# Trainium2, one core: the second block's projection by seven half-width products instead of eight full-width blocks, with weight sums and row scaling on GpSimd

## What is computed

```python
def second_block(x, ...):
    x = x + 0.5 * swiglu(rms_norm(x, ffn1_norm[l]), ...)
    h = rms_norm(x, mix_norm[l])
    proj = h @ w_in[l]                      # 1024 -> 3600 columns
    qkv_a, z_a, a_a, b_a, qkv_b = jnp.split(proj, split_at, axis=-1)
    o_a = gdn_mixer(qkv_a, z_a, a_a, b_a, conv_w[l], ...)   # conv of 5, silu, l2 norm of q and k, delta rule
    o_b = dilated_mixer(qkv_b, q_norm_w[l], k_norm_w[l], rel_bias[l])  # rms norm of q and k, band attention
    x = x + jnp.concatenate([o_a, o_b], axis=-1) @ w_out[l]
    x = x + 0.5 * swiglu(rms_norm(x, ffn2_norm[l]), ...)
```

## Time and the profile before

| | |
|---|---|
| median of three runs | 3348.02 us (3344.82 to 3357.39) |
| the profiled execution, device time | 3344.23 us |
| its span in the trace | 3342.5 us |
| projection stage, first product to first logits | 2383.86 to 2607.40 us |
| PE busy | 3122.7 us, 93% |
| DVE / ACT / POOL busy | 1938.0 / 870.7 / 316.2 us |

### The profile page before, as it was taken

How to read it: one execution, slowest core, us unless ns; L and a number is a source line. 1 busy time by engine, 2 the same in 40 slices (tenths; PEclk the granted TensorE clock), 3 DMA queues, 4 the chain that set the end, 5 groups by cost and what they waited for, 6 DMA issues and landing times.

```text
span 3342.5 us, 72507 instructions
## 1 busy us (share of the span) xinstructions
PE 3122.7 (93%) x28246; PEld 2282.4 (68%) x28247; DVE 1938.0 (58%) x3738; ACT 870.7 (26%) x1541; POOL 316.2 (9%) x277
## 2 busy tenths in 40 slices
PE   8998999799989998999699979999999799999997
PEld 5445886577765446885577758888644478588886
DVE  1486674456651676663566677664548666476644
ACT  1116110356651134111466630000111522110000
POOL 1000000322230000001322210000000033000000
PEclk9999999899999999999899979999999999999998
DMA  7110324299952112223599822223253000122231
GB/s 283 62 65 1 126 89 162 110 341 380 376 193 104 56 45 76 89 88 128 193 377 377 337 107 84 87 89 100 93 110 121 12 3 3 55 84 89 89 97 68
DMA packets 83479, 446.85 MB, mean 134 GB/s; under 512 B 19888, under 2 KB 20024, under 8 KB 39616
## 3 DMA queue, kind: packets, MB, share of 16 engines
q1 hardware_dynamic: 55200, 377.51, 30.4%
q0 software_dynamic: 25136, 63.49, 6.0%
q10 hardware_dynamic: 2928, 3.07, 0.3%
HBM read 411.00 MB, written 32.89 MB: 133 GB/s over the span
## 4 chain that ended last, share of the span: by engine, by line
PE 87%; DVE 4%; ACT 4%; issue 3%; DVEq 1%; DMA 1%; POOL 0%; ACTq 0%; POOLq 0%
PE pb L1150 24%; PE pb L724 17%; PE pb L1030 10%; PE pb L891 9%; PE pb L1053 5%; PE pb L931 4%; PE pb L985 3%; PE pb L1466 2%; ACT arena L1494 1%; PE pb L760 1%; PE pb L828 1%; PE pb L871 1%; PE pb L1037 1%; PE pb L1011 1%; PE pb L1342 1%
## 5 line engine op out<-in xcount | busy, mean ns | idle before, releaser
L1150 PE MATMUL pb<-arena,streamed 128*128 128x256 f32 x1952 | 446.9, 381 | 5.8 <-DVE arena L2335 5.0
L1150 PEld LDWEIGHTS pb<-arena,streamed 128*128 128x128 f32 x1952 | 372.8, 191 | 59.0 <-issue 6.3
L1030 PE MATMUL pb<-arena,xT 128*32 x3008 | 351.6, 276 | 18.1 <-issue 11.4
L724 PE MATMUL pb<-xT,streamed 128*128 128x512 f32 x832 | 365.9, 598 | 0.0
L1030 PE MATMUL pb<-streamed,xT 128*32 128x128 f32 x9024 | 354.7, 276 | 5.8 <-issue 5.8
L1030 PEld LDWEIGHTS pb<-arena,xT 128*32 128x32 f32 x3008 | 323.4, 111 | 32.5 <-issue 26.8
L1030 PEld LDWEIGHTS pb<-streamed,xT 128*32 128x32 f32 x9024 | 327.0, 111 | 7.9 <-issue 7.9
L724 PEld LDWEIGHTS pb<-xT,streamed 128*128 128x128 f32 x832 | 158.5, 192 | 198.4 <-issue 198.2
L1620 ACT ACTIVATE streamed<-arena 128x3072 f32 x94 | 260.1, 2767 | 56.4 <-SPq L483 37.8
L1150 PE MATMUL pb<-arena,am 128*128 128x256 f32 x976 | 227.3, 379 | 0.0
L1150 PEld LDWEIGHTS pb<-arena,am 128*128 128x128 f32 x976 | 185.4, 190 | 25.2
(11 more groups left out here) (459 smaller groups left out, 4967.9 us busy)
## 6 DMA issues: line engine op xcount, KB each, us to landing
arena<-in_w_moe SPq DMA_DIRECT2D x192, 1024.0 KB, 9.4
streamed<-in_w_tail SPq DMA_DIRECT2D x87, 1024.0 KB, 5.0
streamed<-in_w_layer SPq DMA_DIRECT2D x78, 1024.0 KB, 4.9
xT<-xs_dram POOLq DMA_DIRECT2D x22, 512.0 KB, 8.5
ys_dram<-xT POOLq DMA_DIRECT2D x88, 128.0 KB, 9.2
xs_dram<-lnw POOLq DMA_DIRECT2D x12, 512.0 KB, 17.7
rel_dram<-xtok POOLq DMA_DIRECT2D x1, 4092.0 KB, 86.7
arena<-rel_dram POOLq DMA_DIRECT2D x1, 3584.0 KB, 15.2
```

The source lines that it names most:

```text
L724: last = mm(pb[bank][:, 0:cols], unit(w, u, k), rhs[:, k * cols:(k + 1) * cols], start=(k == 0), stop=(k == KC - 1))
L1030: last = mm(pb[m][r0:r0 + MOE_BLOCK, 0:FW], rows, w, start=(k == 0), stop=(k == KC - 1))
L1150: last = mm(pb[p][:, 0:HALF], stat(i), mov(i), start=(opens and i == 0), stop=(closes and i == steps - 1))
```

## The change

The projection's 28 groups become 14 pairs, one weight pair each. PE makes seven products a pair, each of four steps with 128x256 inputs: P1 = a11 and P2 = a12 into the halves of bank 0, P3 (weights s2) and P4 (a21, changed in place) into bank 1, P5 (s1) and P6 (s4) into bank 6, P7 (a22) into bank 7. P3 waits for the first and P4 for the second signal of the weight sums.

- POOL forms the weight sums (`in_weights`: four operations of 128x512). They have one set of buffers, so those of pair c+1 wait until P6 of pair c is done. It also multiplies each recombined pair by `rs` (`scale_pair`, 128x1024), which was DVE's L2527. The silu, squares and convolutions wait for it.
- ACT copies the first half bank of each pair (`first_product`), DVE recombines by seven adds of 128x256 (`in_reads`, `in_upper`).
- The input sums are made by DVE inside the last part of the feed-forward (`projection_sums`).
- The norm sums go by batches of four groups: PE makes four products with 32 columns of ones into four row ranges of bank 2, ACT takes the root of one 128x512 tile, DVE one reciprocal of it (`invert`), PE spreads it to banks 2 to 5 by four products over 32 rows, and DVE multiplies by the banks (`apply_norm`). `n_done` counts to 4. The first sums stand in pair 4 between P4 and P5, the first spread in pair 5 at the same place; the further ones follow every second pair.
- The bias table's load `hank` is issued by POOL after `scale_pair(10)` instead of straight behind its store; the store follows `scale_pair(1)`. The copy of v by ACT moves behind the last pair, and PE waits for it ahead of the fourth logits.

On POOL (the DMAs of the bias table stand where the text above says):

```diff
-            pool.wait_ge(n_done, 2)
+            def in_weights(c):
...
+                pool.wait_ge(w_loaded[j % SLOTS], (DEPTH * LAYER_USES + j // SLOTS + 1) * 16)
+                if c:
+                    alone(pool)
+                    pool.wait_ge(prod_ready, IN_PRODS + N_PROD * (c - 1) + 6)
+                add(s1, a21, a22, ALU.add)
+                pool.drain()
+                add(s2, s1, a11, ALU.subtract).then_inc(w_summed, 1)
+                add(a21, a11, a21, ALU.subtract)
+                pool.drain()
+                if c == 0:
+                    pool.wait_ge(sq_summed, 2)
+                add(s4, a12, s2, ALU.subtract).then_inc(w_summed, 1)
...
+            def scale_pair(c):
+
+                pool.wait_ge(prod_read, IN_READS + 4 * c + 4)
+                y = cut(in_pair(c), S)
+                nc.gpsimd.tensor_tensor(y, y, rs.unsqueeze(1).to_broadcast([P, 2, S]), ALU.mult).then_inc(lin_free, 2)
...
+            in_weights(0)
+            for c in range(IN_PAIRS):
+                if c + 1 < IN_PAIRS:
+                    in_weights(c + 1)
+                if c == 0:
+                    pool.wait_ge(ab_scaled, 1)
+                    alone(pool)
+                scale_pair(c)
```

On PE:

```diff
-            pe.wait_ge(dn_free, KC)
+            pe.wait_ge(prod_read, products_read(0, FF_SUMS))
...
-            for g in range(H_AB):
-                linear(pair(AB_SLOT + 1 + g // 2), g % 2, xns[1], DEPTH * LIN_LAYER + g, g % 2)
...
-                    mm(pb[2 + c % 4][:], ones if c < 8 else block_ones, nsq[c % 2], start=True, stop=True).then_inc(nsum_ready, 1)
...
+                b = (g - 8) // 4
+                if g % 4 == 0 and 0 <= b < 4:
+                    pe.wait_ge(rvar, 2)
+                    pe.wait_ge(nsq_ready, 4 * (b + 1))
+                    alone(pe)
+                    if b:
+                        pe.wait_ge(n_done, b)
+                    for q in range(4):
+                        last = mm(pb[SUM_BANK][q * 32:q * 32 + 32, :], ones[:, 0:32] if b < 2 else block_ones[:, 48:80], nsq[q], start=True, stop=True)
+                    last.then_inc(nsum_ready, 1)
+                b = (g - 10) // 4
+                if g % 4 == 2 and 0 <= b < 4:
+                    pe.wait_ge(n_inverse, b + 1)
...
+                    for q in range(4):
+                        r0 = q * 32
+                        last = mm(pb[2 + q][:], (pick_row if b < 2 else pick_rows)[r0:r0 + 32, :], nrm[b][r0:r0 + 32, :], start=True, stop=True)
+                    last.then_inc(n_spread, 1)
...
+                bank_free(0)
+                product(0, 0, a11, part(0, 0))
+                product(0, 1, a12, part(1, 0))
+                pe.wait_ge(w_summed, IN_SUMS + 2 * c + 1)
...
+                product(1, 0, s2, added(1))
+                pe.wait_ge(w_summed, IN_SUMS + 2 * c + 2)
...
+                product(1, 1, a21, added(2))
+                at_group(2 * c)
+                bank_free(2)
+                product(6, 0, s1, added(0))
+                product(6, 1, s4, part(1, 1))
+                sums_ready(4)
+                bank_free(3)
+                product(7, 0, a22, added(3))
+                at_group(2 * c + 1)
```

On ACT, in step g (with silu of group g - 2 between the first piece and the second):

```diff
+            def first_product(c):
+
+                if c:
+                    act.wait_ge(prod_read, IN_READS + 4 * (c - 1) + 2)
+                    alone(act)
+                act.wait_ge(prod_ready, IN_PRODS + N_PROD * c + 2)
+                fn(in_first, pb[0][:, 0:HALF], ACT.Copy).then_inc(first_copied, 1)
...
+                if g % 2 == 0 and 0 < g < H_AB:
+                    first_product(g // 2)
...
+                    if c >= 4:
+                        act.wait_ge(nsum_ready, c // 4)
+                    elif c == 2:
+                        act.wait_ge(rel_ready, 1)
+                    fn(nsq[c % 4], grp(big, c), ACT.Square).then_inc(nsq_ready, 1)
...
+                    act.wait_ge(nsum_ready, b + 1)
+                    fn(nrm[b], pb[SUM_BANK][:], ACT.Sqrt, scale=1.0 if b < 2 else 1.0 / HEAD_DIM, bias=eps).then_inc(nstd, 1)
```

On DVE:

```diff
+            def in_reads(c):
+
+                dve.wait_ge(first_copied, 2 * DEPTH * MIXED + c + 1)
+                alone(dve)
+                out = in_pair(c)
+                p1, u2, u3 = in_first, in_u2, in_u3
+                v.tensor_tensor(out[:, 0:HALF], p1, pb[0][:, HALF:S], ALU.add).then_inc(prod_read, 1)
+                dve.wait_ge(prod_ready, IN_PRODS + N_PROD * c + 4)
+                v.tensor_tensor(u2, p1, pb[1][:, 0:HALF], ALU.add)
+                dve.drain()
+                v.tensor_tensor(u3, u2, pb[1][:, HALF:S], ALU.add).then_inc(prod_read, 1)
+
+            def in_upper(c):
...
+                dve.wait_ge(prod_ready, IN_PRODS + N_PROD * c + 6)
...
+                dve.wait_ge(prod_ready, IN_PRODS + N_PROD * c + 7)
+                v.tensor_tensor(out[:, S:3 * HALF], u3, pb[7][:, 0:HALF], ALU.add).then_inc(prod_read, 1)
...
-                    dve.wait_ge(lin_ready, DEPTH * LIN_LAYER + g + 1)
-                    v.tensor_tensor(grp(big, H_ORDER[g]), pb[g % 2][:], rs, ALU.mult).then_inc(lin_free, 1)
-                    dve.drain()
+                    if g % 2 == 0:
+                        in_reads(g // 2)
+                    else:
+                        in_upper(g // 2)
+                    dve.drain()
...
+                if g - 2 < H_SQ or g in V_AT:
+                    dve.wait_ge(lin_free, DEPTH * LIN_LAYER + 2 * (g // 2) + 2)
+                    alone(dve)
+                    convolve(g - 2 if g - 2 < H_SQ else H_V + V_AT.index(g))
+                b = g // 4 - 2
+                if g % 4 == 1 and 0 <= b < 4:
+                    invert(b)
+                if g % 4 == 3 and 0 <= b < 4:
+                    apply_norm(b)
```

More of the change, by code:

```diff
@@ L277, in two_blocks @@
         ctmp = [pT2[0], pT2[1]]
[L278 to L279 removed]
+        nsq = lg2[0:2] + [am[:, 2 * S:3 * S], am[:, 3 * S:4 * S]]
+        nrm = [am[:, 3072 + (b % 2) * S:3072 + (b % 2 + 1) * S] for b in range(4)]
+        pick_row, pick_rows = am[:, S:S + P], am[:, S + P:S + 2 * P]
         at[0] = 0
@@ L650, in _ @@
-            pool.wait_ge(n_done, 2)
+            def in_weights(c):
+                j = AB_SLOT + 1 + c
+                s1, s2, s4 = in_w
+                w = ring[j % SLOTS]
+                a11, a12, a21, a22 = (w[:, q * S:(q + 1) * S] for q in range(4))
+                add = nc.gpsimd.tensor_tensor
+                pool.wait_ge(w_loaded[j % SLOTS], (DEPTH * LAYER_USES + j // SLOTS + 1) * 16)
[10 more added lines that the diff above has]
+                add(s4, a12, s2, ALU.subtract).then_inc(w_summed, 1)
@@ new lines, in apply_norm @@
+            def apply_norm(b):
+                dve.wait_ge(n_spread, b + 1)
+                for q in range(4):
+                    x = grp(big, 4 * b + q)
+                    last = v.scalar_tensor_tensor(out=x, in0=x, scalar=(P ** -0.5, 1.0, qk_w[:, 0:1], qk_w[:, 1:2])[b], in1=pb[2 + q][:], op0=ALU.mult, op1=ALU.mult)
+                last.then_inc(n_done, 1)
+            def in_reads(c):
[6 more added lines that the diff above has]
+                v.tensor_tensor(u2, p1, pb[1][:, 0:HALF], ALU.add)
+                dve.drain()
+                v.tensor_tensor(u3, u2, pb[1][:, HALF:S], ALU.add).then_inc(prod_read, 1)
@@ new lines, in _ @@
+            picks = identity.rearrange("p (q r) -> p r q", r=32)
+            for r in range(2):
+                v.tensor_reduce(pick_rows[:, r * 64:r * 64 + 1], picks[:, 16 * r, :], AX.X, ALU.add)
+            v.tensor_scalar(qk_w[:, 0:1], qk_w[:, 0:1], HEAD_DIM ** -0.5, None, ALU.mult)
+            dve.drain()
+            v.tensor_copy(pick_row, pick_rows[:, 0:1].to_broadcast([P, P]))
+            for r in range(2):
+                v.tensor_copy(pick_rows[:, r * 64 + 1:r * 64 + 64], pick_rows[:, r * 64:r * 64 + 1].to_broadcast([P, 63]))
```

224 lines of the change are left out of this document (135 added, 89 removed).

## The result

The changed kernel takes 3423.1 us (median of 4 runs, 3422.6 to 3429.0) against 3352.7 us for the kernel before beside it (4 runs): ratio 1.0223, interval 1.0201 to 1.0245. It is slower by 70 us by these two medians and by 75 us by the ratio, where a gain of 20 had been forecast.

A forecast was written before the change was run, and what follows sets the result against it. PE, busy 93% of the span, was taken to bound the kernel; -23.9 - 2.6 - 4.0 - 1 - 1 + 15 = -17.5 us gave 3328 us, with 3314 to 3340 for 8 in 10.

The forecast's parts named there:

- four and two drains 5.4 us ... Cost nothing: GpSimd's weight sums per pair: four additions and two drains take 5.4 us, fit within PE's 6.88 us, cost nothing.
- the bias table's "Nothing": Bias table: store 86.7 us, load 15.2, load issued some 50 us ahead of its use; no cost.
- rival (c): GpSimd's sums miss P4 in every pair, slowed by DVE or long drains; 3354 at 2.1 us an operation; chance 0.1.
- Products: PE in the projection: fourteen pairs of seven 1.72 us products, 168.5 us against 192.4, -23.9 us.
- Norm sums: PE's norm sums and spreads: eight batches at 0.9 us plus 0.5 for shape changes, 11.2 against 13.8, -2.6 us.
- +18 with serial spreads: Upper bound on the norm sums' term, if the spread's four products run one after another at 3.4 us.
- The end: Stage's end: PE's 7.34 us wait for reciprocals goes, 3.3 us of add, scaling and hand-overs replaces it; -4.0 us.
- First and second stall: PE waits 6.8 us before the first norm sum and 6.6 before the first spread, DVE and ACT being late.
- the 12.4 us of a round: DVE's round per pair, adds, two convolutions and waiting for ACT: 12.4 us against PE's 12.04, before stretching by POOL.
- The clock behind the stalls: Lower clock after each stall costs 2 us more, 4 us for both.
- The start: Projection's start: `ab` products no longer wait for `dn_free`; -1 us (0 to -3).
- rival (b): Same stalls but deeper, lag reaching banks 6 and 7, lower clock lasting: another 8 to 12 us, 3338; chance 0.17.

The follow-up runs named there:

- the run with counts: Changed kernel with GpSimd's two drains per pair's weight sums replaced by waits on its additions' count; 0.9966 and, run again, 0.9981 of the kernel before.

## Why the prediction was wrong

**The step that failed** is the one on GpSimd: "four and two drains 5.4 us ... Cost nothing", together with the bias table's "Nothing". I priced a drain by what the engine has to compute and a transfer by who asks for its data. In these runs a drain behind a transfer of GpSimd's own lasted until that had landed: 4.5, 78.5 and 8.1 us of standing in the three pairs that follow an issue, and on PE 75.7 + 5.7 + 1.6 = 83.0 us of waiting. The store's 86.7 us stood in the earlier trace rows, and in GpSimd's program the next pair's sums, drains among them, stand right behind its issue. The forecast named rival (c), GpSimd's sums too late for P4, but as a matter of each operation's length and in every pair.

**The rest of the sum** can be read from the run with counts, stage 218.5 us, where the forecast had 223.5 - 23.9 - 2.6 - 4.0 + 15 = 208.0:

- Products: 1.73 us each, the last pair 12.09: -23.1 for -23.9. Right.
- Norm sums: two pairs with one sum and one spread take 26.63 us (2536.43 - 2509.80), less 24.18 and halved 1.22 a batch: 9.8 for 13.8, -4.0 for -2.6. The spread's four products do share the array (1.07 us). The forecast's upper bound, "+18 with serial spreads", does not follow from its own prices: four serial spreads of 3.4, four sums of 0.9 and eight changes of shape at 0.8 make 23.6, +9.8 against 13.8.
- The end: 3.0 us of waiting for 7.3, -4.3 for -4.0. Right.
- First and second stall: 8.5 and 8.6 us for 6.8 and 6.6, +3.7. The places and the engines were right. The reason given, every pair's convolutions stretched by GpSimd's sums, was mostly not: without the sums 7.9 and 7.0 remain, of which the scaling may have some 2 us each. The larger part was the order of work on ScalarE and VectorE, which I had in the 12.4 us of a round but not as the cause. GpSimd's stretch costs as much in other places: without its sums the stage is 8.9 us and the start 3.9 us shorter.
- A third stall, 3.7 us for the decays' product in pair 3, was not forecast as a wait of PE: +3.7. Of it 2.1 us are VectorE's product of 8 columns standing beside GpSimd's scaling.
- The clock behind the stalls: 4 us for two stalls were forecast, from waits of "2.4 to 4.5 us"; the rows named for it show waits of 3.27 and 7.34. In the timeline of the run with counts (first batch of sums behind its stall and next pair's first product; then the same without a stall)

```profile
2462.97 1.07 PE L1290 MATMUL pb<-arena,cst 128*32 128x512 f32 x2 [8.54 <-issue]
...
2472.09 3.62 PE L1316 MATMUL pb<-arena,streamed 128*128 128x256 f32 x16
...
2503.52 0.62 PE L1290 MATMUL pb<-arena,cst 128*32 128x512 f32 x2
...
2509.80 3.62 PE L1316 MATMUL pb<-arena,streamed 128*128 128x256 f32 x16
```

2472.09 - 2462.97 = 9.12 us against 2509.80 - 2503.52 = 6.28, so 2.8; in the same way 2.4 behind the second stall and 2.9 behind the third: 8.1 us, +4.

These make +0.8 - 1.4 - 0.3 + 3.7 + 3.7 + 4.1 = 10.6 us, and 10.5 are missing.

- The start: -1 was forecast. It is -0.3 in the changed kernel and +2.4 with counts. The changed kernel got off lightly because its first drain kept GpSimd still, behind the small loads, while VectorE finished.

So without the drains' waits the kernel is at 0.997 to 0.998 instead of the forecast's 0.994; its medians of 3339.2 and 3339.6 lie just inside the range of 3314 to 3340, near rival (b)'s 3338. That they lie inside owes something to luck: the third stall and the low clock behind it were in no term, and the reason given for the first two stalls was mostly wrong. For the kernel as it was, slower had been given 0.06.

## What to carry to other kernels

Before a drain is put on GpSimd, look at what that engine has issued and not yet seen land; a count on the operations that must be ordered costs 0.1 us and does not see transfers. In a busy stage, let another engine issue the long transfers, or put them where no drain follows. And where an engine is a little late, first look at what stands ahead of the late operation in its own order: that took 10.7 us out of the stage here with no work less, though 7.5 of them came back behind the logits by the clock, while moving the consumer a step later only moved it behind another convolution.

## What the runs showed of the hardware

- A drain on GpSimd with a transfer of its own under way: 80.07 and 89.17 us, for stores that landed 84.1 and 87.7 us after their issue; with none, 1.4 us, of which 1.3 are the operation ahead. A drain on ScalarE with its own store under way: 3.8 us, no more than the work in it.
- VectorE beside GpSimd's operations: two additions 2.60 us for 1.29 and two products with a column of weights 2.71 for 0.88, beside sums of 512 columns; four convolution steps up to 6.85 for 3.23, beside two sums and a scaling, but 3.23 in eight of twelve; a product of 8 columns 2.31 for 0.16, for as long as GpSimd's scaling of 2.37 lasted.
- After a wait of 1.29 us at one place behind the logits the granted clock stayed at 1.00 in two executions of one kernel and fell to 0.50 for some 16 us in two of another that is the same from there on: 4.5 us for 48 transposes, and 8.0 us up to the products of L1583, which is all of the 7.5 us by which the whole stretch differs.
